# Moving six weight buffers and the rounding remainders by multiples of 32 bytes in a two-layer decoder kernel

## The chip, the cores and the metric

The kernel runs as one program on one core of a Trainium2 chip. The metric is the device time of one execution in microseconds, and the median of three executions stands for the kernel.

## What is computed

The input is x of 256 tokens by 1024 channels in float32. Two layers follow one another.

```python
h = h + hgrn2_mixer(rmsnorm(h), w_in, lb, g_norm, w_out)      # layer 0, gated linear recurrence
h = h + swiglu(rmsnorm(h), w_gate, w_up, w_down)              # layer 0, dense, width 2816
k, v = shared_kv(h, kv_norm, kv_w, k_gain)                    # one projection
h = h + swa_attention(rmsnorm(h), k, v, w_q, q_gain, sink, rel_bias, w_o)   # layer 1
h = h + moe_swiglu(rmsnorm(h), w_router, w_gate, w_up, w_down)              # layer 1, top 2 of 8 experts
```

Every weight matrix is float32. The eight experts have three matrices each, of 1024 by 3584.

## The kernel before

The program has two halves. The **dense half** holds the input projection, the recurrence, its output projection, the dense feed-forward, and the attention. The **expert half** is a loop over work items, each an expert and up to 96 of its tokens.

*The dense half.* All its weights pass as a stream of chunks, each of 128 partitions by 2048 numbers (8 KiB in each partition). SyncE loads chunk c into one of six slots of `raw`. ScalarE rounds it to TensorE's short float32 format into `w_hi`, slot c % 3 (line 626). VectorE subtracts that from the chunk and puts the remainder into `w_lo`, the same slot (line 916). The activations are split in the same manner: the columns' rounded part is `ht_hi`, their remainder is `ht_lo`. (`mid_hi` and `mid_lo` are the pair for the feed-forward's hidden values, `kv_hi` and `kv_lo` the pair for keys and values.) TensorE then forms each product from three matmuls in the short format, lines 1442, 1443 and 1444: high with high, high with low, low with high. A matmul has a stationary operand, which a weight load brings into the array, and a moving one, which streams through it. The program's names stand in the trace with the moving operand first, so `bank<-ht_lo,w_hi` has `ht_lo` moving over `w_hi`.

There are three shapes of dense matmul. `to_features` has a 128x128 block of the weight buffer stationary and 256 columns of the activations moving. `to_rows` has a 128x128 block of activations stationary and the weight buffer moving, 256 columns wide for some chunks and 512 for others. TensorE takes one chunk after another, 48 matmuls for a chunk at 256 columns and 24 at 512; the order is written out by hand. While a matmul's moving operand streams, the stationary operand of the next matmul is loaded. Both are read from the on-chip memory at the same time.

*The expert half.* Each item loads the expert's three matrices through a ring of 28672 numbers a partition, which is a third of an item. It lies partly over `raw` (48 KiB a partition) and partly in `more_ring` (64 KiB). The loop multiplies in plain float32, with the ring's contents moving over 32 stationary columns of `xT` (line 1888) or `hidT` (line 1900), four such products side by side in the array.

*Where things lie.* The buffers are allocated in the order in which `build_program` names them, each after the one before it, with sizes rounded up to 32 bytes. The expert half's buffers start where the dense half's three-slot `w_hi` and `w_lo` start. So an allocation ahead of the weights moves everything behind it. The start addresses within a partition, as built, leave these remainders on division by 128:

```
buffer                                     before    changed
raw, h, ht_hi                                 0         0
ht_lo, xs, const                              0        32
w_hi slots 0, 1, 2                       64, 64, 64   96, 32, 64
w_lo slots 0, 1, 2                       64, 64, 64    0, 32, 96
fT, qT, gT, eT, mid_hi, mid_lo, kv_hi,       64        96
kv_lo, val, og, sc, bias_rev, prs, pTs
more_ring, xT, xr                            64        96
hidT, e_silu, e_hid, hnT                      0        32
```

A slot is 8192 bytes, so all three slots of one buffer had the same remainder. The blocks that the products of lines 1442 to 1444, 1888 and 1900 read start at multiples of 128 bytes from the buffer's start, so such an operand has its buffer's remainder.

Of the kernel before, what the change touches and what calls it, by code (L numbers as in the profile page):

```python
# [9 lines left out]
P = 128  # L10
# [19 lines left out]
CW = 2048  # L30
RAW, SPLIT = 6, 3
# [66 lines left out]
def build_program(nc, a, out):  # L98
    f32, f32r = mybir.dt.float32, mybir.dt.float32r
    i32, u32 = mybir.dt.int32, mybir.dt.uint32  # L100
    ALU, ACT, AX = mybir.AluOpType, mybir.ActivationFunctionType, mybir.AxisListType
    MUL, ADD, SUB = ALU.mult, ALU.add, ALU.subtract

    def plain(ap):
        return ap.bitcast(f32)
# [36 lines left out]
    ctx = ExitStack()  # L142
    with ctx:
        def sb(stack, name, shape, dt=f32):
            return stack.enter_context(nc.sbuf_tensor(name, shape, dt))

        def sem(name):
            return ctx.enter_context(nc.semaphore(name))


        raw = sb(ctx, "raw", [P, RAW, CW])
        h = sb(ctx, "h", [P, TT, D])
        with ExitStack() as over:

            early = sb(over, "early", [P, TT, 2, D])
        ht_hi = sb(ctx, "ht_hi", [P, KT, T], f32r)
        ht_lo = sb(ctx, "ht_lo", [P, KT, T], f32r)
        xs = sb(ctx, "xs", [P, TT, D])
        const = sb(ctx, "const", [P, K_END])
# [24 lines left out]
        early_slot = sb(ctx, "early_slot", [P, TT, 2], u32)  # L184

        dense = ExitStack()
        w_hi = sb(dense, "w_hi", [P, SPLIT, CW], f32r)
        w_lo = sb(dense, "w_lo", [P, SPLIT, CW], f32r)
        s = ExitStack()
        fT = sb(s, "fT", [P, HEADS, T])  # L190
        qT = sb(s, "qT", [P, HEADS, T])
# [49 lines left out]
        slot = sb(ctx, "slot", [P, TT, 2, 4], u32)  # L241
# [39 lines left out]
        hi_ready = sem("hi_ready")  # L281
        split_ready = sem("split_ready")
# [35 lines left out]
        first_hi = sem("first_hi")  # L318
        first_lo = sem("first_lo")
# [73 lines left out]
            return banks[c % 4] if c < 12 else banks[4 + c % 2]  # L393

        def split_view(buf, c, width):
            return buf[:, c % SPLIT, :].rearrange("p (k c) -> p k c", c=width)


        def ring_place(k):
# [211 lines left out]
        def _(act):  # L611
# [9 lines left out]
            def round_chunk(c, slot_raw, raw_count, slot):  # L621
                act.wait_ge(raw_full[slot_raw], raw_count)

                if not (isinstance(c, int) and c < SPLIT):
                    act.wait_ge(chunk_used, c - (SPLIT - 1))
                nc.scalar.activation(w_hi[:, slot, :], raw[:, slot_raw, :], ACT.Copy).then_inc(hi_ready, 1)  # L626

            def round_to(c_last):

                while nxt[0] <= c_last:  # L630
                    c = nxt[0]
                    round_chunk(c, c % RAW, 16 * (c // RAW + 1), c % SPLIT)
                    nxt[0] += 1
# [44 lines left out]
            def round_x(pairs):  # L678
                for u in pairs:
                    act.wait_ge(fresh_turned, u + 1)  # L680
                    for k in range(2):
                        kt = 2 * u + k
                        ins = nc.scalar.activation(ht_hi[:, kt, :], FRESH_1[u][:, T * k:T * k + T], ACT.Copy,
                                                   scale=cols[:, kt:kt + 1])
                    ins.then_inc(fresh_hi, 1)

            half_chunk = lambda buf, part: buf[:, 0, 1024 * part:1024 * part + 1024]
            act.wait_ge(turn_free, 1)
            round_x((0, 1))
            act.wait_ge(first_full, 16)  # L690
            nc.scalar.activation(half_chunk(w_hi, 0), half_chunk(raw, 0), ACT.Copy).then_inc(first_hi, 1)
            round_x((2, 3))
            act.wait_ge(raw_full[0], 16)
            nc.scalar.activation(half_chunk(w_hi, 1), half_chunk(raw, 1), ACT.Copy).then_inc(hi_ready, 1)
            nxt[0] = 1
            round_to(LEAD - 1)
            act.wait_ge(x_loaded[1], 16)
# [7 lines left out]
            for c in range(N_IN):  # L705
# [10 lines left out]
                part, i = divmod(c, 4)  # L716
# [186 lines left out]
        def _(dve):  # L903
# [9 lines left out]
            def rest_chunk(c, slot_raw, slot):  # L913

                dve.wait_ge(hi_ready, c + 1)
                nc.vector.tensor_tensor(w_lo[:, slot, :], raw[:, slot_raw, :], plain(w_hi[:, slot, :]), SUB).then_inc(split_ready, 1)  # L916

            def rest_to(c_last):
                while nxt[0] <= c_last:
                    c = nxt[0]  # L920
                    rest_chunk(c, c % RAW, c % SPLIT)
                    nxt[0] += 1
# [54 lines left out]
            def rest_x(pairs):  # L977
                for u in pairs:
                    dve.wait_ge(fresh_hi, u + 1)
                    for k in range(2):  # L980
                        kt = 2 * u + k
                        ins = nc.vector.scalar_tensor_tensor(
                            out=ht_lo[:, kt, :], in0=FRESH_1[u][:, T * k:T * k + T], scalar=cols[:, kt:kt + 1],
                            in1=plain(ht_hi[:, kt, :]), op0=MUL, op1=SUB)
                    ins.then_inc(fresh_lo, 1)

            half_chunk = lambda buf, part: buf[:, 0, 1024 * part:1024 * part + 1024]
            rest_x((0, 1))
            dve.wait_ge(first_hi, 1)
            nc.vector.tensor_tensor(half_chunk(w_lo, 0), half_chunk(raw, 0), plain(half_chunk(w_hi, 0)), SUB).then_inc(first_lo, 1)  # L990
            rest_x((2, 3))
            dve.wait_ge(hi_ready, 1)
            nc.vector.tensor_tensor(half_chunk(w_lo, 1), half_chunk(raw, 1), plain(half_chunk(w_hi, 1)), SUB).then_inc(split_ready, 1)
            nxt[0] = 1
            rest_to(LEAD - 1)
            turn_copy(cols[:, 16:64], 48)
# [35 lines left out]
            for c in range(N_IN):  # L1032
# [38 lines left out]
                if c == 7:  # L1071
# [6 lines left out]
                    k = 0  # L1078
# [17 lines left out]
                if c in (11, 12, 13):  # L1096
                    j = c - 11
                    k = sum(NCH - 1 - jj for jj in range(j))
# [330 lines left out]
            for t in range(TT):  # L1429
                for half in range(2):  # L1430
                    part = h[:, t, 512 * half:512 * half + 512]
# [4 lines left out]
        def _(pe):  # L1436
# [50 lines left out]
            def to_features(c, bank, hi, lo, fresh=None):  # L1487

                pe.wait_ge(split_ready, c + 1)
                wh, wl = split_view(w_hi, c, 256), split_view(w_lo, c, 256)  # L1490
                for half in range(2):
                    for k in range(KT):
                        if half == 0 and fresh is not None and k in fresh:
                            pe.wait_ge(fresh_lo, fresh[k])
                        cut = slice(P * half, P * half + P)
                        ins = product(bank[:, 256 * half:256 * half + 256], (wh[:, k, cut], wl[:, k, cut]),
                                      (hi[:, k, :], lo[:, k, :]), k == 0, k == KT - 1)
                ins.then_inc(chunk_used, 1)
# [464 lines left out]
```

## Time and profile before

| | us |
|---|---|
| median of three executions | 1325.21 |
| lowest and highest of them | 1322.11, 1326.4 |
| span of the profiled execution | 1321.3 |
| TensorE busy in it | 1299.1 (98%) |
| VectorE busy | 360.1 (27%) |
| ScalarE busy | 246.4 (19%) |

The profiled execution is known by its span, from its first to its last instruction. The times of the three executions also hold what lies around the span. Against the median this is 1325.21 - 1321.3 = 3.9 us.

Times in the profile are microseconds unless marked ns. A group of instructions is given by its line, engine, operation and operands. Matmuls are pipelined: one starts long before the one ahead of it has ended, so a matmul's duration is longer than the distance from its start to the next start. That distance, here called the step, is what a matmul costs when TensorE is never idle.

### The profile page before, as it was taken

How to read it: one execution, taken by the hardware profiler on the slowest of the kernel's cores; microseconds unless marked ns; L12 is line 12 of the kernel's file. 1: busy time of each engine (PE TensorE's matmuls, PEld its weight loads, DVE VectorE, ACT ScalarE, POOL GpSimd, SP SyncE). 2: the span in 40 equal slices, each digit the busy share in tenths (PEclk: the TensorE clock that was granted, in tenths of full speed). 3: DMA queues.
4: the chain of work that ended last, by engine and by line, in shares of the span. 5: the costliest groups of instructions: out<-in, count | busy, mean ns of one | idle time of the engine just before them, and what ended most of it. 6: DMA issues, size and time to landing. Idle time of an engine off the chain costs nothing.

```text
span 1321.3 us, 32549 instructions
## 1 busy us (share of the span) xinstructions
PE 1299.1 (98%) x14662; PEld 879.8 (67%) x14662; DVE 360.1 (27%) x539; ACT 246.4 (19%) x370; POOL 56.0 (4%) x50
## 2 busy tenths in 40 slices
PE   8999999999899999999999999999999999999998
PEld 8998899988767533555745655665574575566565
DVE  5875555554875401000000100100100010010011
ACT  5554544443743100000000000000000000000000
POOL 1001000000000320000000000000000000001600
PEclk9999999999999899999999999999999999999999
DMA  9866555565522899999999999999999999999992
GB/s 321 269 210 225 185 182 177 187 223 191 184 96 72 360 421 420 415 419 418 416 419 419 418 418 418 418 410 419 419 404 420 418 407 418 416 409 414 419 413 110
DMA packets 114199, 442.52 MB, mean 335 GB/s; under 512 B 9284, under 2 KB 55700, under 8 KB 83348
## 3 DMA queue, kind: packets, MB, share of 16 engines
q1 hardware_dynamic: 107904, 424.75, 81.5%
q10 hardware_dynamic: 4820, 11.53, 2.5%
q0 software_dynamic: 1344, 4.20, 0.8%
q8 instruction: 120, 1.97, 0.6%
q14 instruction: 11, 0.09, 0.0%
HBM read 434.12 MB, written 12.08 MB: 338 GB/s over the span
## 4 chain that ended last, share of the span: by engine, by line
PE 93%; DVE 3%; ACT 2%; issue 1%; DMA 0%; ACTq 0%; DVEq 0%
PE bank L1888 44%; PE bank L1900 22%; PE bank L1442 8%; PE bank L1444 8%; PE bank L1443 8%; PE bank L1689 1%; PE bank L1600 1%; DVE w_lo L916 1%; ACT w_hi L626 0%; PE bank L1865 0%; DMA const<-in_shape_constants 0%; ACT ht_hi L654 0%; PE bank L1744 0%; PE bank L1940 0%; DVE q_from L1100 0%
## 5 line engine op out<-in xcount | busy, mean ns | idle before, releaser
L1888 PE MATMUL bank<-more_ring,xT 128*32 128x512 f32 (+1 forms) x3456 | 341.0, 545 | 0.0
L1888 PEld LDWEIGHTS bank<-more_ring,xT 128*32 128x32 f32 x3456 | 164.2, 110 | 163.5 <-issue 84.4
L1888 PE MATMUL bank<-raw,xT 128*32 128x384 f32 (+1 forms) x2688 | 259.3, 532 | 0.7 <-DVE xT L1352 0.7
L1888 PEld LDWEIGHTS bank<-raw,xT 128*32 128x32 f32 x2688 | 122.4, 110 | 127.0 <-issue 76.6
L1411 DVE TENSOR_TENSOR e_hid<-e_silu,bank 128x384 f32<-128x384 f32 (+1 forms) x48 | 26.9, 616 | 542.3 <-PE bank L1888 542.3
L1900 PE MATMUL bank<-more_ring,hidT 128*32 128x256 f32 x3072 | 171.4, 379 | 0.0
L916 DVE TENSOR_TENSOR w_lo<-raw,w_hi 128x2048 fp32r<-128x2048 f32 x62 | 141.5, 2289 | 99.1 <-ACT w_hi L626 99.0
L1900 PEld LDWEIGHTS bank<-more_ring,hidT 128*32 128x32 f32 x3072 | 120.8, 110 | 46.4
L1442 PE MATMUL bank<-ht_hi,w_hi 128*128 128x256 f32 x464 | 129.4, 279 | 1.5 <-DVE ht_lo L930 1.5
L1900 PE MATMUL bank<-raw,hidT 128*32 128x256 f32 x2304 | 129.9, 379 | 0.0
L1444 PE MATMUL bank<-ht_hi,w_lo 128*128 128x256 f32 x464 | 128.9, 278 | 0.0
L1443 PE MATMUL bank<-ht_lo,w_hi 128*128 128x256 f32 x464 | 128.9, 278 | 0.0
L626 ACT ACTIVATE w_hi<-raw 128x2048 fp32r<-128x2048 f32 x62 | 118.6, 1918 | 38.7 <-PE bank L1444 38.3
L1900 PEld LDWEIGHTS bank<-raw,hidT 128*32 128x32 f32 x2304 | 91.0, 110 | 37.9 <-issue 0.6
L889 ACT ACTIVATE e_silu<-bank 128x384 f32<-128x384 f32 (+1 forms) x48 | 22.6, 544 | 392.8 <-PE bank L1888 392.8
L1442 PEld LDWEIGHTS bank<-ht_hi,w_hi 128*128 128x128 f32 x464 | 87.9, 189 | 2.5 <-issue 2.4
L1443 PEld LDWEIGHTS bank<-ht_lo,w_hi 128*128 128x128 f32 x464 | 87.9, 189 | 0.0
L1444 PEld LDWEIGHTS bank<-ht_hi,w_lo 128*128 128x128 f32 x464 | 87.9, 189 | 0.0
L892 ACT ACTIVATE yb<-bank 96x512 f32<-96x512 f32 x8 | 4.7, 593 | 441.6 <-PE bank L1900 441.6
L1442 PE MATMUL bank<-w_hi,ht_hi 128*128 128x256 f32 (+1 forms) x224 | 74.4, 332 | 3.7 <-DVE ht_lo L944 1.6
L1444 PE MATMUL bank<-w_hi,ht_lo 128*128 128x256 f32 (+1 forms) x224 | 73.2, 327 | 0.0
L1443 PE MATMUL bank<-w_lo,ht_hi 128*128 128x256 f32 (+1 forms) x224 | 72.9, 326 | 0.0
(284 smaller groups left out, 898.6 us busy)
## 6 DMA issues: line engine op xcount, KB each, us to landing
more_ring<-in_moe_w_up SPq DMA_DIRECT2D x64, 1024.0 KB, 16.2
more_ring<-in_moe_w_down SPq DMA_DIRECT2D x64, 1024.0 KB, 16.9
raw<-in_moe_w_gate SPq DMA_DIRECT2D x64, 768.0 KB, 15.5
more_ring<-in_moe_w_up SPq DMA_DIRECT2D x64, 768.0 KB, 15.8
raw<-in_moe_w_gate SPq DMA_DIRECT2D x48, 1024.0 KB, 16.1
raw<-in_moe_w_down SPq DMA_DIRECT2D x48, 1024.0 KB, 17.5
more_ring<-in_moe_w_gate SPq DMA_DIRECT2D x16, 1024.0 KB
raw<-in_hgrn_w_in SPq DMA_DIRECT2D x15, 1024.0 KB, 11.8
```

The source lines that it names most:

```text
L626: nc.scalar.activation(w_hi[:, slot, :], raw[:, slot_raw, :], ACT.Copy).then_inc(hi_ready, 1)
L889: nc.scalar.activation(e_silu[:, j, 0:w], banks[j][:, 0:w], ACT.Silu).then_inc(e_silu_ready, 1)
L892: nc.scalar.activation(yb[:, 0:512], banks[6][0:CAP, :], ACT.Copy)
L916: nc.vector.tensor_tensor(w_lo[:, slot, :], raw[:, slot_raw, :], plain(w_hi[:, slot, :]), SUB).then_inc(split_ready, 1)
L1411: nc.vector.tensor_tensor(e_hid[:, j, 0:w], e_silu[:, j, 0:w], banks[GRPS + j][:, 0:w], MUL).then_inc(e_hid_ready, 1)
L1442: nc.tensor.matmul(dst, st[0], mv[0], start=first, stop=False)
L1443: nc.tensor.matmul(dst, st[0], mv[1], start=False, stop=False)
L1444: return nc.tensor.matmul(dst, st[1], mv[0], start=False, stop=last)
L1600: whole = lambda bank_rows, at, w, st, mv: nc.tensor.matmul(bank[bank_rows:bank_rows + CH, at:at + w], st, mv, start=True, stop=True)
L1689: nc.tensor.matmul(LOGIT_BANKS[g % 2][b][:, :], const[:, K_ANTI:K_ANTI + P], bias_rev[:, GRP * g:GRP * g + GRP, :][:, heads, 2 * P - P * ( ...
L1888: ins = nc.tensor.matmul(out_banks[j][GTOK * c:GTOK * c + GTOK, 0:w], xT[:, j, kt, :], chunk[:, c], start=kt == 0, stop=kt == KT - 1)
L1900: ins = nc.tensor.matmul(banks[6 + j // 2][GTOK * c:GTOK * c + GTOK, 256 * (j % 2):256 * (j % 2) + 256], hidT[sup][:, g, m, :], ring_place ...
```

## The change

It allocates one unused buffer of 32 bytes ahead of `ht_lo`, makes each of the six slots of the weight split a buffer of its own, and puts unused gaps of 64, 32, 64, 32 and 64 bytes between them. The accesses to the slots are rewritten to match. No instruction is added, removed or moved on any engine, and no size, wait or signal differs; the addresses do.

```diff
         ht_hi = sb(ctx, "ht_hi", [P, KT, T], f32r)
+        sb(ctx, "ht_gap", [P, 8])
         ht_lo = sb(ctx, "ht_lo", [P, KT, T], f32r)
...
         dense = ExitStack()
-        w_hi = sb(dense, "w_hi", [P, SPLIT, CW], f32r)
-        w_lo = sb(dense, "w_lo", [P, SPLIT, CW], f32r)
+        w_hi, w_lo = [], []
+        for place, (buf, gap) in enumerate(zip([w_hi] * SPLIT + [w_lo] * SPLIT, (0, 16, 8, 16, 8, 16))):
+            if gap:
+                sb(dense, f"w_gap{place}", [P, gap])
+            buf.append(sb(dense, f"w_split{place}", [P, CW], f32r))
...
         def split_view(buf, c, width):
-            return buf[:, c % SPLIT, :].rearrange("p (k c) -> p k c", c=width)
+            return buf[c % SPLIT][:, :].rearrange("p (k c) -> p k c", c=width)
...
-                nc.scalar.activation(w_hi[:, slot, :], raw[:, slot_raw, :], ACT.Copy).then_inc(hi_ready, 1)
+                nc.scalar.activation(w_hi[slot][:, :], raw[:, slot_raw, :], ACT.Copy).then_inc(hi_ready, 1)
...
-                nc.vector.tensor_tensor(w_lo[:, slot, :], raw[:, slot_raw, :], plain(w_hi[:, slot, :]), SUB).then_inc(split_ready, 1)
+                nc.vector.tensor_tensor(w_lo[slot][:, :], raw[:, slot_raw, :], plain(w_hi[slot][:, :]), SUB).then_inc(split_ready, 1)
```

## Rows read from the trace of the kernel before

**Rows 1.** The page: busy times, slices of the span, chain that ended last

```profile
PE 1299.1 (98%) x14662; PEld 879.8 (67%) x14662; DVE 360.1 (27%) x539; ACT 246.4 (19%) x370; POOL 56.0 (4%) x50
...
PEclk9999999999999899999999999999999999999999
...
PE 93%; DVE 3%; ACT 2%; issue 1%; DMA 0%; ACTq 0%; DVEq 0%
```

**Rows 2.** Busy time by stretch: us, PE, PEld, DVE, ACT, POOL, clock, DMA share, GB/s

```profile
200.00:300.00 100.00, 100.00 (x749) 94.41 (x749) 55.85 (x43) 43.72 (x33) 0.00 (x0) 1.00 0.59 197
...
550.00:900.00 350.00, 350.00 (x4646) 204.91 (x4638) 26.62 (x47) 15.14 (x33) 0.00 (x0) 1.00 1.01 417
```

**Rows 3.** The chain that ended last, in order of time: the second expert item

```profile
552.83 72.49 PE bank L1888 x767
625.57 36.01 PE bank L1900 x666
```

**Rows 4.** Groups by line and shape (count, busy us, mean ns of one)

```profile
L1443 PE MATMUL bank<-ht_lo,w_hi 128*128 128x256 f32 x464 | 128.9, 278 | 0.0
...
L1443 PE MATMUL bank<-w_lo,ht_hi 128*128 128x512 f32 x96 | 37.5, 390 | 0.0
...
L1443 PE MATMUL bank<-w_lo,ht_hi 128*128 128x256 f32 x128 | 35.4, 277 | 0.0
...
L1443 PE MATMUL bank<-w_lo,mid_hi 128*128 128x512 f32 x88 | 34.3, 389 | 0.0
...
L1443 PE MATMUL bank<-w_lo,kv_hi 128*128 128x256 f32 x32 | 9.1, 283 | 0.0
```

**Rows 5.** Instructions in order of time (start, length), TensorE, to_features, 200.17 to 205.27

```profile
200.17 0.28 PE L1442 MATMUL bank<-ht_hi,w_hi 128*128 128x256 f32 x1
200.28 0.28 PE L1443 MATMUL bank<-ht_lo,w_hi 128*128 128x256 f32 x1
...
205.27 0.28 PE L1442 MATMUL bank<-ht_hi,w_hi 128*128 128x256 f32 x1
```

**Rows 6.** The same view, to_rows at 256 columns, ht stationary, 93.76 to 95.41

```profile
93.76 0.28 PE L1442 MATMUL bank<-w_hi,ht_hi 128*128 128x256 f32 x1
...
95.41 0.28 PE L1444 MATMUL bank<-w_hi,ht_lo 128*128 128x256 f32 x1
```

**Rows 7.** The same view, to_rows at 256 columns, kv stationary, 332.86 to 335.14

```profile
332.86 0.28 PE L1443 MATMUL bank<-w_lo,kv_hi 128*128 128x256 f32 x1
...
335.14 0.28 PE L1444 MATMUL bank<-w_hi,kv_lo 128*128 128x256 f32 x1
```

**Rows 8.** The same view, to_rows at 512 columns, mid stationary, 290.03 to 292.30

```profile
290.03 0.39 PE L1443 MATMUL bank<-w_lo,mid_hi 128*128 128x512 f32 x1
...
292.30 0.39 PE L1444 MATMUL bank<-w_hi,mid_lo 128*128 128x512 f32 x1
```

**Rows 9.** The same view, to_rows at 512 columns, ht stationary, 128.11 to 130.85

```profile
128.11 0.39 PE L1444 MATMUL bank<-w_hi,ht_lo 128*128 128x512 f32 x1
...
130.85 0.39 PE L1444 MATMUL bank<-w_hi,ht_lo 128*128 128x512 f32 x1
```

**Rows 10.** Plain float32 at 512 columns: six merged (timeline), then one line's durations

```profile
365.95 2.74 PE L1689 MATMUL bank<-bias_rev,const 128*128 128x512 f32 x6
...
L1689 PE MATMUL bank<-bias_rev,const x24: 590/592/595, 366.0 to 395.5; 128*128 128x512 f32 x24
```

**Rows 11.** Expert half, groups by line and shape: the ring's two parts

```profile
L1888 PE MATMUL bank<-raw,xT 128*32 128x384 f32 x1536 | 130.1, 487 | 0.7 <-DVE xT L1352 0.7
L1888 PE MATMUL bank<-more_ring,xT 128*32 128x384 f32 x1536 | 129.4, 486 | 0.0
```

**Rows 12.** DMA issues of the expert half: count, size, median us to landing

```profile
more_ring<-in_moe_w_down SPq DMA_DIRECT2D x64, 1024.0 KB, 16.9
raw<-in_moe_w_gate SPq DMA_DIRECT2D x64, 768.0 KB, 15.5
```

More of the change, by code:

```diff
@@ L685, in round_x @@
                     ins.then_inc(fresh_hi, 1)
-            half_chunk = lambda buf, part: buf[:, 0, 1024 * part:1024 * part + 1024]
+            half_chunk = lambda buf, part: buf[:, 1024 * part:1024 * part + 1024]
             act.wait_ge(turn_free, 1)
@@ L690, in _ @@
             act.wait_ge(first_full, 16)
-            nc.scalar.activation(half_chunk(w_hi, 0), half_chunk(raw, 0), ACT.Copy).then_inc(first_hi, 1)
+            nc.scalar.activation(half_chunk(w_hi[0][:, :], 0), half_chunk(raw[:, 0, :], 0), ACT.Copy).then_inc(first_hi, 1)
             round_x((2, 3))
             act.wait_ge(raw_full[0], 16)
-            nc.scalar.activation(half_chunk(w_hi, 1), half_chunk(raw, 1), ACT.Copy).then_inc(hi_ready, 1)
+            nc.scalar.activation(half_chunk(w_hi[0][:, :], 1), half_chunk(raw[:, 0, :], 1), ACT.Copy).then_inc(hi_ready, 1)
             nxt[0] = 1
@@ L985, in rest_x @@
                     ins.then_inc(fresh_lo, 1)
-            half_chunk = lambda buf, part: buf[:, 0, 1024 * part:1024 * part + 1024]
+            half_chunk = lambda buf, part: buf[:, 1024 * part:1024 * part + 1024]
             rest_x((0, 1))
             dve.wait_ge(first_hi, 1)
-            nc.vector.tensor_tensor(half_chunk(w_lo, 0), half_chunk(raw, 0), plain(half_chunk(w_hi, 0)), SUB).then_inc(first_lo, 1)
+            nc.vector.tensor_tensor(half_chunk(w_lo[0][:, :], 0), half_chunk(raw[:, 0, :], 0), plain(half_chunk(w_hi[0][:, :], 0)), SUB).then_inc(first_lo, 1)
             rest_x((2, 3))
             dve.wait_ge(hi_ready, 1)
-            nc.vector.tensor_tensor(half_chunk(w_lo, 1), half_chunk(raw, 1), plain(half_chunk(w_hi, 1)), SUB).then_inc(split_ready, 1)
+            nc.vector.tensor_tensor(half_chunk(w_lo[0][:, :], 1), half_chunk(raw[:, 0, :], 1), plain(half_chunk(w_hi[0][:, :], 1)), SUB).then_inc(split_ready, 1)
             nxt[0] = 1
```

## The prediction

> **What bounds the kernel now.** I read the page first, for who is busy and who ends the chain; then the stretches, for where; then the steps between matmuls, since a change of addresses alone can act only through how long one instruction takes. TensorE is busy 98% of the span and holds 93% of the chain, at the full clock nearly throughout [rows 1]. In a dense stretch it is busy 100.00 of 100 us, while VectorE has 55.85 and ScalarE 43.72 and the loads move 197 GB/s [rows 2]. In the expert loop it is again busy all the time, with 417 GB/s moved [rows 2]. One item is 72.49 + 36.01 = 108.5 us, with no other engine in its chain [rows 3]. So the time is a sum of steps of matmuls. VectorE, ScalarE and the dense loads may all become somewhat slower or faster at no cost: they have at least 44% of the dense stretch free.
>
> **What one matmul costs, and by what it varies.** The short format's columns run at 2.4 GHz, so 256 columns are 106.7 ns and 512 are 213.3 ns.
> - 256 columns, one operand at remainder 0 and the other at 64: 45 steps in 5.10 us, 113.3 ns each [rows 5].
> - The same remainders, another chunk: 14 steps in 1.65 us, 117.9 ns [rows 6]. Four chunks of the span, 192 matmuls, stay in this second state from their first matmul to their last; the rest stay at 113.3.
> - 256 columns, both operands at 64: 19 steps in 2.28 us, 120.0 ns [rows 7].
> - 512 columns, both at 64: 10 steps in 2.27 us, 227.0 ns [rows 8].
> - 512 columns, 64 with 0: 12 steps in 2.74 us, 228.3 ns [rows 9].
> - Plain float32, half the column rate: 5 steps in 2.74 - 0.59 = 2.15 us, 430 ns for 512 columns at 426.7 [rows 10]. That is 3.3 ns beside the columns.
>
> So a dense matmul loses between 6.6 and 15.0 ns over its columns where a plain one loses 3.3, and the loss differs between chunks of one shape, with the operands' remainders or with the moment at which a chunk starts. The two reads that run together, the moving operand and the next stationary one, must get in each other's way. A rule speaks against this reading. The Trainium skill, "TensorE: Matmul & The Clock Gate", section on what happens when you issue a matmul, says that TensorE has two independent read ports and that loading the next weights takes no read bandwidth from the running matmul. By that rule addresses cannot matter and the sum is 0, 1325.2 us. The trace does not agree: one shape of matmul, on an engine that is never idle, has three steps, 113.3, 117.9 and 120.0 ns [rows 5 to 7].
>
> **The change part by part.** No instruction, wait, transfer or size changes. What changes is remainders. Before, every pair of overlapping dense reads starts 64 apart (ht with w) or equal (mid and kv with w). No row has operands 32 apart, so its price has to be bounded. Below lies the plain loss of 3.3 ns, which makes 110.0 ns and 216.6 ns. Above lies the costliest 256-column row, 120.0 ns. My value for unequal remainders is that of the rows with unequal ones, 113.3 and 228.3, the nearest there is; equal ones get 120.0 and 227.0.
>
> 1. *Products of ht with w, 256 columns.* The count is 3 x (464 + 128) + 48 for the first chunk = 1824 matmuls (464 and 128 in [rows 4]). The overlapping pairs are ht_hi with w_hi, ht_lo with w_lo, and ht_hi with the next w_hi. In slots 0, 1, 2 these are now (0,96) (32,0) (0,96); (0,32) (32,32) (0,32); (0,64) (32,96) (0,64). One of nine is equal, none was. 203 x 6.7 ns = **+1.4 us**.
> 2. *kv with w.* 96 matmuls, all equal before. The keys' chunk lies in slot 2 and keeps one pair in three equal, the values' chunk in slot 1 keeps none. 80 x 6.7 ns = **-0.5 us**.
> 3. *mid with w, 512 columns.* 264 matmuls, all equal before; slot 0 keeps two in three, slot 2 one in three, slot 1 none. 176 become unequal, at 1.3 ns: **+0.2 us**. *ht with w, 512 columns*: 288, of which 32 become equal: 0.0.
> 4. *The second state.* It costs 192 x 4.6 ns = 0.9 us. Whether a chunk falls into it depends on more than the remainders. I take half of it as gone, **-0.4 us**; the ends are 0 and -0.9.
> 5. *The expert loop.* `more_ring` goes from 64 to 96, `xT` likewise, `hidT` from 0 to 32, `raw` stays. The two parts of the ring, at 0 and at 64, have means of 487 and 486 ns [rows 11], and 84 groups of four in 36.01 us are 428.7 ns against 426.7 of columns. A move by 64 costs nothing here, and I take the same for 32: 0. If that is wrong, nothing covers it (rivals).
> 6. *Loads and splitting.* Landings in both parts of the ring take 15.5 to 16.9 us [rows 12], so the target's remainder shows no effect; and where VectorE or ScalarE change by a few per cent, the free 44% hides it. If that cover were gone, 5% of VectorE's 55.85 us would be 2.8 us per 100 us.
>
> The sum is 1.4 - 0.5 + 0.2 - 0.4 = +0.7 us, 1321.3 + 0.7 = 1322.0 us of span. The profiled span stands 3.9 us under the median, which lies outside of what changes, so the forecast is 1325.2 + 0.7 = **1325.9 us**, no change. About 0.3%, 4.0 us, is what a measurement of this kernel can tell from none.
>
> **The rivals.**
> - *The reads come apart (faster).* If 32 bytes is a distance at which the two reads miss one another, the dense steps fall toward 110.0 and 216.6 ns. All of it is worth 1824 x 3.3 + 192 x 4.6 + 96 x 10.0 + 264 x 10.4 + 288 x 11.7 ns = 6.0 + 0.9 + 1.0 + 2.7 + 3.4 = 14.0 us. Half of it, 7.0 us, gives 1318.2 us. For it: all pairs now stand at multiples of 64, none shows the plain loss, and the change breaks that for most pairs. Against: there is no row at a distance of 32. It counts as faster when more than 2 of 7 of the loss goes.
> - *More chunks in the dearer state (slower).* The trace has the same operands at 113.3 and at 117.9, and 89% of the 1824 sit in the cheap state. New distances may give all of them the dear one: 1632 x 6.7 + 192 x 2.1 ns = 10.9 + 0.4 = 11.3 us, 1336.5 us. It ends slower from a mean of 2.2 ns for each of the 1824. For it: the present state is near the low end of what is seen at 256 columns. Against: the loss at 64 apart and at 0 apart differs by 6.7 ns only.
> - *The expert loop's matmuls start off a 64-byte place (slower).* An item has 96 + 84 groups, each streamed twice, so 8 items have 2880 streams. At 0 to 6.7 ns each this is 0 to 19 us; at the plain 3.3 ns it is 9.5 us, 1334.7 us. For it: nothing there lies off 64 today. Against: plain float32 streams at half the rate and loses 2 ns a group now.
> - *The ring's loads fall behind.* The loop needs 44.0 MB an item, 407 GB/s, and 417 are moved [rows 2]. A load is issued a third of an item, 36 us, ahead and lands in 17 at most [rows 12]. That leaves 19 us over the whole loop. 5% less rate would cost 5.7 x 8 - 19 = 27 us, 1352 us.
> - *The change does not move what it says.* The built addresses exclude it. That addresses do not act at all is within the forecast.
>
> **How the numbers follow.** Forecast 0.38, with its own range 1322 to 1329. Reads apart 0.32. Dearer state 0.17, expert matmuls 0.10, loads 0.03. So faster is 0.32, same 0.38, slower 0.30. The range reaches to 11 us of the 14 possible below and to the dearer state above: 1314 to 1337 us. Outside are the last of the gain (0.07), the loads (0.03), and slow cases that come together (0.08).
>
> **What would show it.** Right: steps of line 1443 at 113 to 120 ns in all slots, kv below 120.0, item times of 108.5 us. A mean of `bank<-ht_lo,w_hi` under 277 ns or over 280, where it is 278 now [rows 4], would tell the first or second rival; a down phase over 36.1 us the third; idle time of TensorE on loads the fourth. I would be wrong if the span's difference lay in the dense half by more than 4 us, or anywhere in the loop.

## The result and the profile after

| | before | changed |
|---|---|---|
| median of five executions, us | 1325.21 | 1332.92 |
| lowest and highest, us | 1322.11, 1326.41 | 1331.0, 1337.18 |
| span of the profiled execution, us | 1321.3 | 1333.3 |

The ratio is 1.0069, with a 95% interval of 1.005 to 1.0089: the change makes the kernel 7.7 us slower.

The page of the changed kernel, busy times and the chain by engine:

```profile
PE 1311.9 (98%) x14662; PEld 1066.1 (80%) x14662; DVE 360.2 (27%) x539; ACT 246.0 (18%) x370; POOL 56.1 (4%) x50
...
PE 94%; DVE 3%; ACT 2%; issue 1%; DMA 0%; ACTq 0%; DVEq 0%
```

TensorE is busy 12.8 us longer, and the span grew by 12.0 us. VectorE and ScalarE are unchanged. So the bound is the one of [rows 1], and TensorE's own instructions have become longer.

The same stretches as in [rows 2], and two items of the expert loop in the chain, to set beside [rows 3]:

```profile
200.00:300.00 100.00, 100.00 (x755) 95.57 (x754) 54.68 (x41) 41.65 (x32) 0.00 (x0) 1.00 0.57 189
550.00:900.00 350.00, 350.00 (x4713) 288.25 (x4708) 26.62 (x47) 13.89 (x30) 0.00 (x0) 1.00 1.01 416
```

```profile
563.27 72.31 PE bank L1892 x766
635.57 36.04 PE bank L1904 x667
```

In the dense stretch TensorE is still never idle and the clock is full, but its loads bring 189 GB/s where they brought 197: the stream follows TensorE, and TensorE is slower. An item of the expert loop takes 72.31 + 36.04 = 108.35 us, where one took 108.5. The whole loop takes 869.0 us against 868.8. The part from the first product to the loop takes 441.2 us against 432.4, which is 8.8 of the 12.0 us. The other 3 lie at the two ends of the execution: the first product starts 1.5 us later and the last stores end some 1.5 us later.

Not all of this is the change's. The 8.8 us are 7.5 us from the first product to the end of the last (427.4 us against 419.9), and 1.3 in the routing stage behind it, which holds no product of the weight stream. The granted clock fell there in both executions, and lower on average in the changed one, 0.63 against 0.74, with a part of the stage at 1.2 GHz in place of 2.4. In the columns of [rows 2], before and changed:

```profile
431.57:444.11 12.54, 11.27 (x99) 7.80 (x97) 7.20 (x30) 2.78 (x4) 2.92 (x4) 0.74 0.86 337
440.61:454.42 13.81, 12.89 (x98) 9.24 (x97) 7.21 (x30) 2.78 (x4) 2.93 (x4) 0.63 0.87 346
```

At the start, sixteen transposes of x took 3.65 us where they took 1.97. They did the same in `e8_all256` below (3.67 us), which is not slower than the kernel before, and not in `e2_rest_only` (1.97), which is. So this is a difference between executions and not the change's:

```profile
6.48 1.97 PE L1541 MATMUL bank<-const,h 128*128 128x128 f32 x16
6.87 3.65 PE L1545 MATMUL bank<-const,h 128*128 128x128 f32 x16
```

The changed kernel's profiled execution took 1335.09 us, 2.2 above its median. What is left for the products, 7.5 us, agrees with the 7.7 between the medians.

The groups by line and shape, to set beside [rows 4]:

```profile
L1447 PE MATMUL bank<-ht_lo,w_split 128*128 128x256 f32 x464 | 131.3, 283 | 0.0
...
L1447 PE MATMUL bank<-w_split,ht_hi 128*128 128x512 f32 x96 | 37.7, 393 | 0.0
...
L1447 PE MATMUL bank<-w_split,ht_hi 128*128 128x256 f32 x128 | 35.9, 281 | 0.0
...
L1447 PE MATMUL bank<-w_split,mid_hi 128*128 128x512 f32 x88 | 34.5, 392 | 0.0
```

A mean of one rises from 278 to 283 ns, from 390 to 393, from 277 to 281 and from 389 to 392. In order of time, three chunks of `to_features` in slots 0, 1 and 2, first and last matmul of each (the last one of a chunk frees its slot):

```profile
175.22 0.28 PE L1446 MATMUL bank<-ht_hi,w_split 128*128 128x256 f32 x1
...
180.76 0.28 PE L1448 MATMUL bank<-ht_hi,w_split 128*128 128x256 f32 x1
180.87 0.28 PE L1446 MATMUL bank<-ht_hi,w_split 128*128 128x256 f32 x1
...
186.62 0.28 PE L1448 MATMUL bank<-ht_hi,w_split 128*128 128x256 f32 x1
186.74 0.28 PE L1446 MATMUL bank<-ht_hi,w_split 128*128 128x256 f32 x1
...
192.17 0.28 PE L1448 MATMUL bank<-ht_hi,w_split 128*128 128x256 f32 x1
```

Each has 47 steps: 5.54, 5.75 and 5.43 us, that is 117.8, 122.3 and 115.6 ns, where the trace before had 113.3 in every slot at this place. The next three chunks, in the same slots, have 116.7, 118.5 and 118.0, and the six values repeat from then on. For the feed-forward's 512 columns, where [rows 8] had 227.0:

```profile
295.24 0.40 PE L1447 MATMUL bank<-w_split,mid_hi 128*128 128x512 f32 x1
...
300.59 0.39 PE L1446 MATMUL bank<-w_split,mid_hi 128*128 128x512 f32 x1
```

23 steps in 5.35 us are 232.6 ns. Over all steps that follow one another without a break:

| product (count of steps) | before, ns | changed, ns | sum, us |
|---|---|---|---|
| `to_features`, ht over w, 256 (1440) | 113.7 | 118.1 | +6.3 |
| `to_rows`, w over ht, 256 (384) | 114.4 | 118.2 | +1.5 |
| `to_rows`, w over ht, 512 (286) | 229.4 | 232.2 | +0.8 |
| `to_rows`, w over mid, 512 (263) | 226.9 | 231.8 | +1.3 |
| `to_rows`, w over kv, 256 (96) | 120.0 | 117.8 | -0.2 |

The sum is +9.7 us, against the 7.5 by which this stretch grew and the 7.7 of the medians. A part is hidden where TensorE waits for others: its idle time in the stretch fell from 13.8 to 12.3 us. The place of the loss is settled by this. What is open is what about the addresses does it.

### The profile page after: what moved, and what is told of

Read it like the earlier page. It is cut to its first block, busy times and chain, and to the rows that moved or that the text cites. A ratio compares the mean times of both kernels' runs of the same rounds, so it can differ in the third digit from the quotient of the medians.

```text
span 1333.3 us, 32549 instructions
## 1 busy us (share of the span) xinstructions
PE 1311.9 (98%) x14662; PEld 1066.1 (80%) x14662; DVE 360.2 (27%) x539; ACT 246.0 (18%) x370; POOL 56.1 (4%) x50
## 4 chain that ended last, share of the span: by engine, by line
PE 94%; DVE 3%; ACT 2%; issue 1%; DMA 0%; ACTq 0%; DVEq 0%
PE bank L1892 43%; PE bank L1904 22%; PE bank L1446 8%; PE bank L1447 8%; PE bank L1448 8%; PE bank L1693 1%; PE bank L1604 1%; DVE w_split L920 1%; ACT w_split L630 0%; PE bank L1869 0%; DMA const<-in_shape_constants 0%; ACT ht_hi L658 0%; PE bank L1840 0%; PE bank L1748 0%; PE bank L1944 0%
## 5 line engine op out<-in xcount | busy, mean ns | idle before, releaser
L1892 PEld LDWEIGHTS bank<-more_ring,xT 128*32 128x32 f32 x3456 | 232.3, 110 | 96.2 <-issue 7.4
L1892 PEld LDWEIGHTS bank<-raw,xT 128*32 128x32 f32 x2688 | 171.9, 110 | 78.2 <-issue 22.1
L920 DVE TENSOR_TENSOR w_split<-raw,w_split 128x2048 fp32r<-128x2048 f32 x62 | 141.6, 2290 | 105.0 <-ACT w_split L630 105.0
L1446 PE MATMUL bank<-ht_hi,w_split 128*128 128x256 f32 x464 | 131.0, 282 | 1.5 <-DVE ht_lo L934 1.5
L1447 PE MATMUL bank<-ht_lo,w_split 128*128 128x256 f32 x464 | 131.3, 283 | 0.0
L1448 PE MATMUL bank<-ht_hi,w_split 128*128 128x256 f32 x464 | 130.2, 281 | 0.0
L630 ACT ACTIVATE w_split<-raw 128x2048 fp32r<-128x2048 f32 x62 | 118.4, 1913 | 44.5 <-PE bank L1448 44.5
L1904 PEld LDWEIGHTS bank<-raw,hidT 128*32 128x32 f32 x2304 | 116.7, 110 | 12.2
L1446 PEld LDWEIGHTS bank<-ht_hi,w_split 128*128 128x128 f32 x464 | 88.0, 190 | 2.4 <-issue 2.4
L1447 PEld LDWEIGHTS bank<-ht_lo,w_split 128*128 128x128 f32 x464 | 88.0, 190 | 0.0
L1448 PEld LDWEIGHTS bank<-ht_hi,w_split 128*128 128x128 f32 x464 | 87.9, 189 | 0.0
L1446 PE MATMUL bank<-w_split,ht_hi 128*128 128x256 f32 (+1 forms) x224 | 75.0, 335 | 3.6 <-DVE ht_lo L948 1.6
L1448 PE MATMUL bank<-w_split,ht_lo 128*128 128x256 f32 (+1 forms) x224 | 74.0, 330 | 0.0
L1447 PE MATMUL bank<-w_split,ht_hi 128*128 128x256 f32 (+1 forms) x224 | 73.6, 329 | 0.0
```

The source lines that it names most:

```text
L630: nc.scalar.activation(w_hi[slot][:, :], raw[:, slot_raw, :], ACT.Copy).then_inc(hi_ready, 1)
L920: nc.vector.tensor_tensor(w_lo[slot][:, :], raw[:, slot_raw, :], plain(w_hi[slot][:, :]), SUB).then_inc(split_ready, 1)
L1446: nc.tensor.matmul(dst, st[0], mv[0], start=first, stop=False)
L1447: nc.tensor.matmul(dst, st[0], mv[1], start=False, stop=False)
L1448: return nc.tensor.matmul(dst, st[1], mv[0], start=False, stop=last)
L1892: ins = nc.tensor.matmul(out_banks[j][GTOK * c:GTOK * c + GTOK, 0:w], xT[:, j, kt, :], chunk[:, c], start=kt == 0, stop=kt == KT - 1)
```

## The experiments

Three theories. **Distance**: the step depends on how far apart the two operands start that are read together. **Off-64**: an operand whose start is not a multiple of 64 bytes is read more slowly, whatever the other. **Mixture**: it costs that the three pairs of a product, which had one distance, now have several. Below, d is the start of the moving operand less the start of the stationary one, modulo 256 bytes. Before, the starts modulo 256 were 128 for ht and 192 for w, mid and kv. So `to_features` had d = 192, `to_rows` with ht had 64, and with mid and kv 0.

### The step against both starts

`m1_table` is a kernel of its own that leaves the whole decoder out. It writes sixteen moving and five stationary operands, each start 32 bytes further modulo 256 than the one before it, and runs every pair 24 times with nothing else on TensorE.

```python
src = sb("src", [P, 768])
sb("place", [P, PLACE])      # PLACE and AWAY are 8
mv = [sb("mv" + c, [P, 768 + 8], f32r) for c in LETTERS]
sb("away", [P, AWAY])
st = [sb("st" + c, [P, 128 + 8], f32r) for c in LETTERS]
...
for j in STATIONARY:           # 0 to 4
    for i in range(16):
        run(mv[i], st[j], 256, 24)
```

> A kernel of its own that leaves the whole decoder out: runs of 24 short-format matmuls of 256 columns, and runs of 12 of 512, with the moving operand at one start address and the stationary one at another, over start addresses that differ by 32 bytes. Distance theory (two reads that run together disturb each other, by the difference of their start addresses): the step depends on the difference alone, and at differences of 32 or 96 modulo 128 it is 117 to 119 ns, at 0 or 64 it is 113 to 120 ns, as in the kernels. Off-64 theory (an operand that does not start at a multiple of 64 is dearer in itself): 113 ns where both start at multiples of 64, about 118 where either does not, whatever the difference. Mixture theory (the price comes from changing from one remainder to another between chunks): one step for all pairs, apart from the first few matmuls of a run.

The first stationary operand in order of time, with start, total of the 24, and moving operand. `stA` starts at 192, `mvB` at 192 (d = 0), and each next one 32 further:

```profile
32.11 3.04 PE L63 MATMUL bank<-mvB,stA 128*128 128x256 f32 x24
34.98 3.00 PE L63 MATMUL bank<-mvC,stA 128*128 128x256 f32 x24
37.81 2.99 PE L63 MATMUL bank<-mvD,stA 128*128 128x256 f32 x24
40.65 3.03 PE L63 MATMUL bank<-mvE,stA 128*128 128x256 f32 x24
43.51 3.01 PE L63 MATMUL bank<-mvF,stA 128*128 128x256 f32 x24
46.36 2.98 PE L63 MATMUL bank<-mvG,stA 128*128 128x256 f32 x24
49.18 2.89 PE L63 MATMUL bank<-mvH,stA 128*128 128x256 f32 x24
51.91 3.00 PE L63 MATMUL bank<-mvI,stA 128*128 128x256 f32 x24
54.74 3.04 PE L63 MATMUL bank<-mvJ,stA 128*128 128x256 f32 x24
...
71.81 2.90 PE L63 MATMUL bank<-mvP,stA 128*128 128x256 f32 x24
```

A step is the total less the last matmul's own 0.28 us, over 23: 120.0 ns for `mvB`, 113.5 for `mvH`. `mvJ`, 256 bytes after `mvB`, is like it again, and `mvP` like `mvH`. With the other four stationary operands the values move along with them. The steps in ns, from the last ten matmuls of a run at 256 columns and the last four at 512:

| d | 0 | 32 | 64 | 96 | 128 | 160 | 192 | 224 |
|---|---|---|---|---|---|---|---|---|
| 256 columns | 120.0 | 117.6 | 117.7 | 120.1 | 118.6 | 117.4 | **113.3** | 117.8 |
| 512 columns | **226.7** | 233.2 | 229.0 | 234.3 | 233.3 | 233.2 | 233.2 | 233.3 |

Behind the cheap value of 192 there is a second one. Of the ten runs at d = 192 eight settle at 113.3 ns, seven of them within four steps, and two stay at 117.8 for all 24. One of these, and the run of the same stationary operand 256 bytes further:

```profile
74.55 2.99 PE L63 MATMUL bank<-mvA,stB 128*128 128x256 f32 x24
...
97.28 2.89 PE L63 MATMUL bank<-mvI,stB 128*128 128x256 f32 x24
```

2.71 us over 23 steps are 117.8 ns, 2.61 us are 113.5. So 192 allows the cheap state and does not force it. At no other multiple of 32 does a run of this kernel reach it.

One distance in eight is cheap at 256 columns here, and it is the one that the kernel before had in `to_features`. At 512 columns 0 is the cheapest, which mid had. A misaligned start costs nothing by itself: `mvI` and `mvG`, off a 64-byte place, and `mvD` and `mvF`, on one, lie between 117.4 and 118.6 ns.

The Trainium skill, "TensorE: Matmul & The Clock Gate", section on what happens when you issue a matmul, has two independent read ports, so that loading the next tile's weights does not steal read bandwidth from the running matmul. With it every cell of a row would be alike. The cells of the first row differ by up to 6.8 ns at the same clock and the same shape, so for this format the measurement decides against it.

### All buffers 32 bytes further

`e1_all32` is the kernel before with a gap ahead of everything. All starts are off a 64-byte place, no distance changes.

```diff
+        sb(ctx, "raw_gap", [P, 8])
         raw = ...
```

> The kernel before with one unused buffer of 32 bytes ahead of all others, so that every buffer moves by 32 and all distances stay. Distance theory: as before, 1325 +- 2 us, steps of line 1444 at 113.3 ns and 117.9 in few chunks. Off-64 theory: all dense operands are off 64, at least as slow as the changed kernel, 1333 us or more, and the expert loop may show it too. Mixture theory: as before, 1325 us.

```profile
L1444 PE MATMUL bank<-ht_lo,w_hi 128*128 128x256 f32 x464 | 128.3, 277 | 0.0
```

1324.17 us against 1323.56, ratio 1.0004 (0.9994 to 1.0015), and steps of 113.8, 114.4, 229.4, 226.9 and 119.8 ns, all as before. The off-64 theory falls. So does the worry about the expert loop, whose operands all started off a 64-byte place here.

### The change in two halves

`e2_rest_only` moves `ht_lo` alone, and puts what lies behind it back to where it lay modulo 256. `e3_slots_only` is the changed kernel with its first gap behind `ht_lo`, so that only the slots are spread.

```diff
 e2, against the kernel before
+        sb(ctx, "ht_gap", [P, 8])
         ht_lo = sb(ctx, "ht_lo", [P, KT, T], f32r)
+        sb(ctx, "back_gap", [P, 56])
 e3, against the changed kernel
-        sb(ctx, "ht_gap", [P, 8])
         ht_lo = sb(ctx, "ht_lo", [P, KT, T], f32r)
+        sb(ctx, "ht_gap", [P, 8])
```

> The kernel before with only ht_lo at remainder 32 (224 bytes of padding behind it keep all later remainders). It touches one overlapping pair in three of the products of ht with w: at to_features the moving ht_lo over the load of w_lo, at to_rows the load of ht_lo. Distance theory: those matmuls go from 113.3 to about 118, and the following ones may be drawn along: between a third (+3 us, 1328) and all (+8 us, 1333). Off-64 theory: a third, +3 us, 1328. Mixture theory: within a chunk the pairs now differ, +3 to +8 us as well.

> The changed kernel with ht_lo back at remainder 0, all else at the changed addresses. Distance theory: slots 0 and 1 are 32 from a multiple of 64 for every pair but w_lo of slot 0, slot 2 only for w_lo: half to two thirds of the loss, +4 to +6 us, 1329 to 1331; slot 2's pair ht_hi with w_hi (0 with 64) at 113 ns. Off-64 theory: the same size, as w_split0, 1, 4 and 5 are off 64. Mixture theory: the whole loss, +8 us, 1333.

Of e2 the three lines of the `to_features` product:

```profile
L1445 PE MATMUL bank<-ht_lo,w_hi 128*128 128x256 f32 x464 | 131.5, 283 | 0.0
L1444 PE MATMUL bank<-ht_hi,w_hi 128*128 128x256 f32 x464 | 131.3, 283 | 1.5 <-DVE ht_lo L932 1.5
L1446 PE MATMUL bank<-ht_hi,w_lo 128*128 128x256 f32 x464 | 129.4, 279 | 0.0
```

Either half has the whole loss: e2 1332.79 us, ratio 1.0075 (1.0061 to 1.0089), and e3 1333.55, ratio 1.0073 (1.0056 to 1.0091). For e3 the distance theory had asked for half to two thirds of it, and that was a miss. So the halves do not add up. In e2 one pair in three left the cheap distance, 192 for 224, and the mean step of all three went to 118.9 ns. The product as a whole, not the pair, is cheap or dear. That is what the mixture theory says too, so the next kernels take it apart.

### Finer distances, and pairs in a mixture

`m2_fine` is again without the decoder. It moves one operand in steps of 4 bytes, runs the three pairs of a product at distances (a, b, a) with a and b any of the eight, and puts runs at one distance behind runs at another.

```python
for o in range(64):
    run([(mv[o % 16], st[0], o)], 256, 24)
...
for high in range(8):
    for low in range(8):
        run([(mv[2], st[(8 - high) % 8], 0), (mv[2], st[(8 - low) % 8], 0), (mv[2], st[(8 - high) % 8], 0)], 256, 36)
```

> A kernel of its own, without the decoder: the same short-format matmuls with (1) the moving operand's start moved in steps of 4 bytes over 256 (256 columns) and of 8 bytes (512 columns), (2) runs of 36 whose overlapping reads stand at two distances in the order of the kernel (high, low, high), for 8 by 8 distances, (3) runs at each distance that follow a run at distance 192 or at distance 0. Theory of distance modulo 256: at multiples of 32 it repeats the first table (113.4 ns at 192, 117.5 to 120.4 elsewhere). If the reads meet in lines of 16 bytes, nothing changes within 16 bytes; a step of 109 to 110 ns somewhere would show a placement better than any multiple of 32. Mixed distances 192 and 224: if each pair pays for itself 115.0 ns, if the timing is drawn along up to 119. History: a run at distance 64 stays at 113.3 ns behind one at 192 and takes 117.7 behind one at 0, as the chunks of the kernel before did.

Four of the fine distances, 16, 112, 188 and 192 bytes:

```profile
39.74 2.88 PE L63 MATMUL bank<-mvE,stA 128*128 128x256 f32 x24
...
108.28 2.92 PE L63 MATMUL bank<-mvM,stA 128*128 128x256 f32 x24
...
162.58 3.04 PE L63 MATMUL bank<-mvP,stA 128*128 128x256 f32 x24
165.46 2.90 PE L63 MATMUL bank<-mvA,stA 128*128 128x256 f32 x24
```

The cheap value is 113.3 ns at 16, 144 and 192 bytes, and at 112 from the ninth step on, and nowhere is it lower. 188 bytes are at 120.0, and the others lie between 115.6 and 123.3. In mixtures (192, 192) took 113.3, (192, 64) 113.5 and (64, 192) 113.3, while (64, 64) took 117.8, (192, 224) 117.7 and (192, 160) 122.2. What ran ahead changes little: distance 64 took 117.7 behind 192 and 117.8 behind 0, and over all eight distances the two differ by 1.0 ns at most. So one pair at another distance mostly loses the cheap state for all three, as in e2, and a few mixtures keep it. At 512 columns the table did not repeat at its best place: in runs of ten, distance 0 swung between 224 and 236 ns and did not reach 226.7. The lowest means of a run's last four steps were 229.5 at 64 bytes and 230.0 at 56 and 248.

### Distances without a mixture

Three kernels move the weights' split and all behind it, so that every pair of a product has one new distance. They differ from the kernel before by one gap each.

```diff
         dense = ExitStack()
+        sb(dense, "w_gap", [P, 8])      # e4; 48 in e5, 32 in e6
         w_hi = sb(dense, "w_hi", [P, SPLIT, CW], f32r)
```

> The kernel before with one 32-byte gap ahead of w_hi: ht stays, all six slots and the stage's buffers move by 32, the expert half stays. No mixture between slots or between high and low. Distance theory with the first table: ht over w at 160 costs 117.5 ns (+5.5 us over 1440 matmuls), w over ht at 96 120 ns (+2.1 us), at 512 columns 234 ns (+1.3 us), mid and kv as before: +8.9 us, 1332.5. Mixture theory: nothing, 1323.6.

> The kernel before with 192 bytes ahead of w_hi: every dense operand at the same remainder modulo 256, all at multiples of 128. Distance theory: 120.0 ns for all matmuls of 256 columns (+9.1 us for ht moving, +2.1 us for w moving), 226.7 ns for all of 512 (-0.8 us): +10.4 us, 1334.0. Off-64 and mixture theories: nothing, 1323.6.

> The kernel before with 128 bytes ahead of w_hi: all remainders modulo 128 stay, the distance of ht to w goes from 192 to 64 modulo 256. If the period is 256 as the first table says: ht over w 117.7 ns (+5.8 us), w over ht at 192 113.4 ns (-0.4 us), at 512 columns 233.7 ns (+1.2 us): +6.6 us, 1330.2; less where a chunk stays in the cheap state. If the period is 128 or less: nothing, 1323.6.

The kernel before took 1324.36 us beside these three. "Table" stands for the values of `m1_table`.

| | `to_features` d: table, measured | `to_rows` 256 d: table, measured | `to_rows` ht 512: table, measured | us | ratio (95%) |
|---|---|---|---|---|---|
| e4, +32 | 160: 117.4, 118.6 | 96: 120.1, 120.0 | 96: 234.3, 233.4 | 1332.57 | 1.0067 (1.0054 to 1.008) |
| e5, +192 | 0: 120.0, 120.0 | 0: 120.0, 120.0 | 0: 226.7, 227.8 | 1331.91 | 1.0056 (1.0044 to 1.0068) |
| e6, +128 | 64: 117.7, 117.6 | 192: 113.3, 114.0 | 192: 233.2, 233.3 | 1329.55 | 1.0044 (1.0028 to 1.0059) |

```profile
L1444 PE MATMUL bank<-ht_lo,w_hi 128*128 128x256 f32 x464 | 130.3, 281 | 0.0
```

```profile
L1444 PE MATMUL bank<-ht_lo,w_hi 128*128 128x256 f32 x464 | 131.9, 284 | 0.0
```

```profile
L1444 PE MATMUL bank<-ht_lo,w_hi 128*128 128x256 f32 x464 | 129.7, 280 | 0.0
```

These are the groups of e4, e5 and e6. Nine values from the table, none more than 1.2 ns off, in kernels with no mixture in them: the mixture theory is not needed for the loss. e5 has every operand of these products at a multiple of 128 bytes, and it costs about as much as the change does. e6 keeps every remainder modulo 128, and costs 5.2 us. (One of e6's six executions took 6084.1 us. The ratio leaves it out, and nothing here shows why it was so long.) The whole of e6 is in d: it exchanged the distances of `to_features` and `to_rows`, and with them went the cheap state. In order of time, 48 matmuls of `to_rows` and 48 of `to_features` in e6:

```profile
70.79 0.28 PE L1443 MATMUL bank<-w_hi,ht_hi 128*128 128x256 f32 x1
...
76.12 0.28 PE L1445 MATMUL bank<-w_hi,ht_lo 128*128 128x256 f32 x1
...
183.48 0.28 PE L1443 MATMUL bank<-ht_hi,w_hi 128*128 128x256 f32 x1
...
189.02 0.28 PE L1445 MATMUL bank<-ht_hi,w_lo 128*128 128x256 f32 x1
```

47 steps take 5.33 us (113.4 ns) in the first and 5.54 us (117.9 ns) in the second. One chunk of each goes the other way: the second of `to_features` has 113.3 ns at d = 64, and the seventh of `to_rows` 117.7 at d = 192.

### A better place for kv, and two controls

`e7b_kv` moves the kv pair by 2112 bytes, 64 modulo 256, to d = 192. `e8_all256` moves all behind `ht_hi` by 256 bytes, which by the distance theory changes nothing. `e9_lo128` moves `w_lo` alone by 128 bytes, which makes the mixtures (192, 64) in `to_features` and (64, 192) in `to_rows`.

```diff
 e7b
+        sb(kvs, "kv_gap", [P, 528])
...
-        over_kv = sb(s, "over_kv", [P, 2 * KT * T])
+        over_kv = sb(s, "over_kv", [P, 2 * KT * T + 528])
 e8
+        sb(ctx, "ht_gap", [P, 64])
         ht_lo = sb(ctx, "ht_lo", [P, KT, T], f32r)
 e9
+        sb(dense, "lo_gap", [P, 32])
         w_lo = sb(dense, "w_lo", [P, SPLIT, CW], f32r)
+        sb(dense, "back_gap", [P, 32])
```

> The one placement that the table says is better than the kernel before: kv_hi and kv_lo 2112 bytes further, so that w over kv stands at distance 192 modulo 256 in place of 0, all else as before. Distance theory: the 96 matmuls of lines 1442 to 1444 with kv go from 120.0 to 113.3 ns, -0.6 us, which the trace shows and the time (0.05%) does not: 1323.7 +- 2. Rival, that only ht and w matter or that the position in memory matters: 120.0 ns stays.

> The kernel before with a gap of 256 bytes ahead of ht_lo in place of the change's 32: ht_lo and everything behind it move, all distances modulo 256 stay. Distance theory modulo 256: as before, steps of ht over w 113.3 to 113.7 ns on average, 1324 +- 2 us. A period longer than 256, or that moving ht_lo away from ht_hi is itself the cause: 117 to 119 ns, 1329 to 1333.

> The kernel before with w_lo alone 128 bytes further (and 128 behind it, so that the stage's buffers keep their remainder): high pairs at distance 192, low pairs at 64. By the table of mixed runs (113.5 ns for high 192 with low 64, 113.3 for high 64 with low 192) the two mixtures cost nothing at 256 columns: 1440 matmuls at 113.5, 384 at 113.3 to 114; at 512 columns mid's pairs stand at 0 and 128 and may lose up to 2 ns on 264 matmuls, +0.5 us: 1324 to 1325. Rival, that any difference between the high pair and the low pair is dear (as 192 with 224 was in e2): 117 to 118 ns, +6 us, 1330.

*e7b*: 1323.08 us against 1325.41, ratio 0.9992 (0.998 to 1.0005). The kv steps fall from 120.0 to a mean of 115.7 ns: the keys' chunk stays at 117.8, the values' comes to 113.4 and 114.0, the two states of d = 192 once more. At 96 matmuls that is 0.4 us, below what a measurement can tell. It is the best place found. It beats the changed kernel, and cannot be told from the one before.

*e8*: 1324.32 us, ratio 0.9987 (0.9976 to 0.9998), so 256 bytes more do no harm. But its trace shows the two states again, at d = 192. Two stretches of 48 matmuls of `to_features`, with the operands in the same places modulo 256:

```profile
44.22 0.28 PE L1443 MATMUL bank<-ht_hi,w_hi 128*128 128x256 f32 x1
...
49.76 0.28 PE L1445 MATMUL bank<-ht_hi,w_lo 128*128 128x256 f32 x1
...
185.72 0.28 PE L1443 MATMUL bank<-ht_hi,w_hi 128*128 128x256 f32 x1
...
191.05 0.28 PE L1445 MATMUL bank<-ht_hi,w_lo 128*128 128x256 f32 x1
```

47 steps take 5.54 us in the one and 5.33 us in the other, 117.9 and 113.4 ns. The first sixteen chunks, up to 111 us, are in the dear state here, and nearly all of the later feed-forward's in the cheap one. Before, four chunks were dear: the first of all, the last two 256-column chunks with ht stationary, and one of the feed-forward. Among e8's dear ones are all eight 256-column chunks with ht stationary, at d = 64, six of which had 113.3 ns before: so d = 64 has two states as well. The state may differ between executions of one kernel, since e8's profiled execution, 1328.05 us, lies 3.7 us above its median, and 13 more dear chunks of 48 matmuls at 4.5 ns are 2.8 us. That is an argument and not shown, since one execution of each kernel has a trace.

*e9*: 1326.19 us, ratio 1.0012 (1.0002 to 1.0022). `to_features` at the mixture (192, 64) stays at 113.4 ns, as in the table of mixtures. `to_rows` at (64, 192) takes 117.8, where that table has 113.3. And 512 columns over mid, with only the middle pair moved to 128, rise from 226.9 to 231.5 ns, where 2 ns at most were expected. The kv steps, at (0, 128), come to 117.8 where the table of mixtures has 119.3. So that table tells the kernel's steps only in part.

## Why the prediction was right and where it was wrong

The range held: 1332.92 us lies in 1314 to 1337. It held by its width of 23 us, drawn so that it reached the second rival. The case that came is that rival, *more chunks in the dearer state*, given 0.17 and 1336.5 us. The forecast itself, no change at 1325.9 us, was 7.0 us off, and the text's own sign of being wrong came true: the dense half holds more than 4 us of the difference.

- **What bounds the kernel** was right: the time is a sum of TensorE's steps, and the difference between the medians is in them. That the step depends on where two operands lie to each other, against the rule, was right as well (`m1_table`). That it is their reads which meet is the explanation the text gave for it; no run looks at the reads themselves.
- **Step 1, ht with w at 256 columns**, is the step that failed. It asked whether remainders modulo 128 are equal, and gave unequal ones "that of the rows with unequal ones, 113.3 and 228.3, the nearest there is". The quantity is the signed distance modulo 256, and 113.3 is the better price of one in eight of its values, 192. Of the rest none is under 117.4. Forecast +1.4 us; measured 6.3 + 1.5 = 7.8. The evidence stood in [rows 5 to 7], three prices for one shape. The text used the spread as bounds, but the value in between as if it were typical, when it was the lowest price seen.
- **Step 2, kv**: -0.5 against -0.2 us. The direction was right, by luck: at 256 columns d = 0, with 120.0 ns, is one of the two dearest multiples of 32.
- **Step 3, 512 columns**: +0.2 and 0.0 against +1.3 and +0.8. Here 0 is the cheapest distance, so leaving it costs 5 ns and not 1.3.
- **Step 4, the second state**: half of 0.9 us was taken as gone. Instead all 256-column chunks with ht left the cheap state, to 115.6 to 122.3 ns. The term's own note, that a chunk's state depends on more than the remainders, holds: it is what the ten runs at d = 192 show.
- **Steps 5 and 6** were right: the expert loop 868.8 and 869.0 us, VectorE 360.1 and 360.2, ScalarE 246.4 and 246.0. `e1_all32` shows it for starts that are all off 64.
- **The 3.9 us under the median** do not all lie outside the span. In the changed kernel's profiled execution time and span are 1335.09 - 1333.3 = 1.8 us apart. The other 2 us are most likely the distance of one execution from the median. The forecast does not depend on it, since it sets +0.7 us on the median.
- **The rivals.** *More chunks in the dearer state* had the mechanism and nearly the size: 11.3 us were worked out, since all 1824 were to go to 120.0 ns, and they went to 118.1. Its mark, a mean of `bank<-ht_lo,w_hi` over 280 ns, came as 283. Against it the text said that the loss at 64 and at 0 differs by 6.7 ns only; but 6.7 ns for 1824 matmuls is the 3 in 1000 three times over. *The reads come apart* assumed that the plain float32 loss, 110.0 ns, can be reached. No distance of `m2_fine` goes below 113.3, so its 14.0 us never existed. *Expert matmuls off a 64-byte place* and *the ring's loads* did not occur, with 416 GB/s against 417. The price of the second was also overstated: its 27 us took 5% off the rate that is needed and not off the 417 GB/s that are moved, which would leave 396 and cost some 3 us.

What the distance explains of the changed kernel: `to_features` in slots 0, 1, 2 stands at (160, 32), (96, 0) and (64, 192), for which the mixtures took 117.8, 117.9 and 113.3 ns. Measured, by chunks that alternate between two values in each slot, are 117.8 and 116.7, 118.5 and 122.3, 115.6 and 118.0. Slot 0 fits, slot 1 in one of its two values; slot 2 does not, nor does `to_rows` of e9 with the same mixture.

**Open.** What puts a run into the cheap or the dear state where both occur; the distance of the run ahead is not it (`m2_fine`). Why `to_rows` at d = 64 reaches 113.3 in six chunks of the kernel before, where no run of the table at 64 does and e8 has none. In the traces before, of e1 and of e7b these six follow chunks at 113.3 without a break and the next one, behind a break, is at 117.8, while in e8 they follow chunks at 117.8; that looks as if a chunk takes over the state of the one ahead, but distance 64 right behind a run at 113.3 took 117.7 in `m2_fine`. Why chunks with the same operands alternate in the changed kernel: the pattern repeats after six chunks, and no run tells whether that comes from the output banks, from the six slots of `raw`, or from what the chunk ahead left. And how the memory serves two reads so that 192 bytes is good: no run here looks at that, only at the sum.

## What to carry to other kernels

When a kernel is a sum of matmuls at one step, compare the step with its columns' time for each pair of operands. Where it differs between pairs of one shape, take the cheapest that you see as a find that a move of any buffer can undo, not as the usual price. A kernel of its own that runs one shape over all distances costs one run and gives the table that no reading of the trace of before can give. An allocation ahead of such operands is a change of speed even where it moves no instruction, and alignment to 64 or 128 bytes is not the measure for it.

## What the runs showed of the hardware

- In the short format the step of back-to-back matmuls, each with its own weight load, depends on the difference of the two operands' starts modulo 256 bytes, from 113.3 to 120.1 ns at 256 columns in multiples of 32 and up to 123.3 in multiples of 4. The order of distances is another one at 512 columns, 226.7 to 234.3 ns in multiples of 32.
- At 256 columns distance 192 has two states that last, 113.3 and 117.8 ns, in one execution and with the same operands. Distance 64 has them too: 113.3 and 117.8 ns in the kernel before. The difference of the starts limits the step and does not fix it.
- 16 bytes are not the smallest unit of it: 0, 4 and 8 bytes took 120.0, 123.3 and 116.7 ns.
- The floor, 113.3 ns, is 17/16 of the columns' 106.7, and 226.7 is 17/16 of 213.3. Why is not shown.
- Plain float32 with 32 stationary columns shows none of it in the loop's time, though the loads of its weights do move. The expert half's largest group of them, before and in the changed kernel:

```profile
L1888 PEld LDWEIGHTS bank<-more_ring,xT 128*32 128x32 f32 x3456 | 164.2, 110 | 163.5 <-issue 84.4
```

```profile
L1892 PEld LDWEIGHTS bank<-more_ring,xT 128*32 128x32 f32 x3456 | 232.3, 110 | 96.2 <-issue 7.4
```

Each takes 110 ns in both, but they overlap one another less and so fill 232.3 us where they filled 164.2. The matmuls that they serve took no longer. A rise of the weight loads' busy share, here from 67% to 80% of the span, is not by itself a cost.
